# Gate and up projections in two groups of 1024 tokens, with the samples' own products and weights loaded in place

## The reference

```
x  = x + concat(A, B) @ w_out                     # one output projection
h2 = rms_norm(x, norm_ffn_w)
g, u = split(h2 @ w_ffn_in)                       # two halves of FF columns: gate and up
gc = conv_b + gp[0:T]*conv_w[0] + gp[1:T+1]*conv_w[1] + gp[2:T+2]*conv_w[2]   # gp: g behind 2 rows of history
x  = x + (silu(gc) * u) @ w_down
```

## Time and profile before

| | us |
|---|---|
| median of 3 runs (lowest, highest) | 2361.06 (2359.53, 2365.66) |
| the profiled execution's own time | 2364.47 |
| its span, first to last instruction | 2362.7 |
| before the positions | 662.4 |
| positions, to the first matmul of gate and up | 662.4 to 887.1 |
| gate and up, first group | 887.1 to 1238.7 |
| second group | 1238.7 to 1590.7 |
| third group, to the first matmul of down | 1590.7 to 1931.4 |
| down | 1931.4 to 2362.7 |

### The profile page before, as it was taken

How to read it: one execution, slowest core, us unless ns; L and a number is a source line. 1 busy time by engine, 2 the same in 40 slices (tenths; PEclk the granted TensorE clock), 3 DMA queues, 4 the chain that set the end, 5 groups by cost and what they waited for, 6 DMA issues and landing times.

```text
span 2362.7 us, 34413 instructions
## 1 busy us (share of the span) xinstructions
PE 2253.2 (95%) x13423; PEld 1984.9 (84%) x13423; DVE 1620.8 (69%) x2271; ACT 899.3 (38%) x1524; POOL 1034.6 (44%) x811
## 2 busy tenths in 40 slices
PE   7999999999999998888879999989999999999999
PEld 6899878887777888777768999988999998888887
DVE  5666655556573457888878899888998974445653
ACT  4555622222232324444444444444444433233331
POOL 4333312222121346655554666655666630245730
PEclk9999999999999998999998999999999999999999
DMA  8433222222154553444344333353333345686454
GB/s 283 151 126 121 79 86 81 81 81 67 45 183 142 192 184 122 156 139 138 132 161 140 117 118 116 118 181 100 119 118 119 119 158 190 219 289 202 139 177 165
DMA packets 208076, 333.95 MB, mean 141 GB/s; under 512 B 23083, under 2 KB 148679, under 8 KB 205847
## 3 DMA queue, kind: packets, MB, share of 16 engines
q1 hardware_dynamic: 207883, 331.69, 41.5%
q0 software_dynamic: 32, 0.07, 0.0%
HBM read 235.42 MB, written 97.24 MB: 141 GB/s over the span
## 4 chain that ended last, share of the span: by engine, by line
PE 65%; DVE 7%; DMA 5%; issue 4%; POOL 3%; ACT 3%; SPq 0%; DVEq 0%; POOLq 0%; ACTq 0%
PE bank L114 12%; PE bank L115 12%; PE bank L116 12%; PE bank L2803 9%; PE bank L2804 8%; PE bank L2805 8%; DMA late_c_raw<-in_w_ffn_in_dram 3%; DVE late_t L3184 1%; DVE late_s_act L3154 1%; DVE late_t_lo L3129 1%; POOL late_c_raw L3381 1%; POOL late_t_raw L3385 1%; DVE late_t L3187 1%; DMA late_a_raw<-h_parts 1%; ACT late_t_hi L2930 1%
## 5 line engine op out<-in xcount | busy, mean ns | idle before, releaser
L2803 PE MATMUL bank<-late_a_hi,late_b_hi 128*128 128x384 f32 (+1 forms) x1056 | 350.0, 331 | 56.3 <-issue 18.6
L2804 PE MATMUL bank<-late_a_lo,late_b_hi 128*128 128x384 f32 (+1 forms) x1056 | 344.7, 326 | 0.0
L2805 PE MATMUL bank<-late_a_hi,late_b_lo 128*128 128x384 f32 (+1 forms) x1056 | 343.2, 325 | 0.0
L2803 PE MATMUL bank<-late_a_hi,late_t_hi 128*128 128x384 f32 (+1 forms) x792 | 262.9, 332 | 19.6 <-DVE late_gp L3172 8.5
L2803 PEld LDWEIGHTS bank<-late_a_hi,late_b_hi 128*128 128x128 f32 x1056 | 201.7, 191 | 69.1 <-issue 36.3
L2804 PE MATMUL bank<-late_a_lo,late_t_hi 128*128 128x384 f32 (+1 forms) x792 | 258.3, 326 | 0.0
L2805 PE MATMUL bank<-late_a_hi,late_t_lo 128*128 128x384 f32 (+1 forms) x792 | 257.6, 325 | 0.0
L114 PE MATMUL bank<-late_e_hi,late_y_a_hi 128*128 128x512 f32 x616 | 242.1, 393 | 2.1 <-DVE late_e_lo L3202 2.1
L116 PE MATMUL bank<-late_e_hi,late_y_a_lo 128*128 128x512 f32 x616 | 242.6, 394 | 0.0
L115 PE MATMUL bank<-late_e_lo,late_y_a_hi 128*128 128x512 f32 x616 | 241.7, 392 | 0.0
L3379 POOL TENSOR_TENSOR late_t_raw<-late_c_raw 128x512 f32<-128x512 f32 x64 | 84.2, 1315 | 327.9 <-DMA late_c_raw<-in_w_ffn_in_dram 300.4
(11 more groups left out here) (380 smaller groups left out, 5187.1 us busy)
## 6 DMA issues: line engine op xcount, KB each, us to landing
late_c_raw<-in_w_ffn_in_dram SPq DMA_DIRECT2D x64, 1024.0 KB, 5.1
late_y_a_raw<-act_parts SPq DMA_DIRECT2D x77, 512.0 KB, 3.6
late_e_raw<-in_w_down_dram SPq DMA_DIRECT2D x77, 256.0 KB, 4.1
act_parts<-late_s_act SPq DMA_DIRECT2D x22, 768.0 KB, 4.4
att_next_hh<-h_parts SPq DMA_DIRECT2D x16, 1024.0 KB, 4.8
late_d_raw<-in_w_down_dram SPq DMA_DIRECT2D x11, 1024.0 KB, 7.6
late_a_raw<-h_parts SPq DMA_DIRECT2D x14, 768.0 KB, 12.7
act_parts<-late_t SPq DMA_DIRECT2D x22, 384.0 KB, 2.5
```

The lines of the kernel that those rows point to most:

```text
L2803: nc.tensor.matmul(out, w_h, hi[:, c, :], start=first, stop=False, skip_group_check=True)
L2804: nc.tensor.matmul(out, w_h, lo[:, c, :], start=False, stop=False, skip_group_check=True)
L2805: ins_ = nc.tensor.matmul(out, w_l, hi[:, c, :], start=False, stop=last, skip_group_check=True)
```

## The change

- `GROUPS` becomes two groups of 1024 prompt tokens, so H = 512 in both, and there are 22 steps and 44 units in place of 33 and 66.
- The samples are no longer columns of the first group. In each of its 22 units `sample_unit` multiplies the unit's weights with the samples' `hs_hi`, `hs_lo` plainly, behind the sixth product: 48 matmuls with 128x128 weights and 64 moving columns, into bank 6. ACT `keep_z` and DVE `add_s` take them out, and convolution, silu and gating of the samples have instructions of their own (`conv_head_s`, `tap_s`, `silu_of_s`, `gate_s`). The result goes to DRAM (`store_as`), and the samples' down projection runs in the second group, six matmuls behind the fifth product of each unit (`down_s`), with `load_as`, `load_ds`, `round_as`, `round_ds`, `split_as` and `split_ds`.
- The weights are loaded into `b_raw[u]`, which shares its memory with `b_lo[u]`. So `load_b(u, next)` waits until the unit that uses it has been multiplied (`prod`, and `prod_s` in the first group), and `split_b` waits for all four sums.
- `t` is single, and `s_act` lies over `up`: `conv_head` and the `keep_first` of u = 1 wait until the step before has been stored.
- `a_hi` of the first group lies over `w_lo` and `w_hi` of the output projection. Its rounding and splitting, seven matrices of 128x2048, move from positions 7 to 15 to the last position and into the first step, behind `w_used` and the last `proj`. `norm_x` of the last position moves behind `split_a` too.
- Tiles are stored and paired from position 9 on (4 pairs in place of 6); `first_a` moves to positions 10 to 13.

The core of the diff:

```diff
-ORDER = (0, 1, 2, 3, NT, 4, 7, 5, 8, 6, 9, 10, 13, 11, 14, 12, 15)
+ORDER = (0, 1, 2, 3, NT, 4, 5, 6, 7, 8, 12, 9, 13, 10, 14, 11, 15)
...
-GROUPS = [Group(0, 0, SAMPLE_AT * P, NS, (0, 2)), Group(1, 512, 768, 0, (2, 5)), Group(2, 1280, 768, 0, (5, 8))]
+GROUPS = [Group(0, 0, SEQ // 2, (0, 4)), Group(1, SEQ // 2, SEQ // 2, (4, 8))]
...
         def load_b(u, r):
             if r is None:
                 return
-            if turn(r) >= 1:
-                w_split(sp, before(r), 4 * u + 3)
+            p = before(r)
+            w_prod(sp, p, 7 * u + 6)
+            if has_s(p):
+                w_prod_s(sp, p, u)
...
+                p = before(r)
+                if r == FIRST:
                     store_s(final)
+                else:
+                    load_b(1, r)
+                if G.index == 1:
+                    load_ds(2 * i)
+                if has_s(p):
+                    store_as(p)
+                if G.index == 1:
+                    load_as(i)
+                store_act(p)
+                if G.index == 1:
+                    load_ds(2 * i + 1)
+                if r == LAST:
+                    load_turn(0)
+                    load_turn(1)
+                load_b(0, after(r))
...
+                if has_s(r) and n == 5:
+                    sample_unit(r, u)
+                if G.index == 1 and n == 4:
+                    down_s(2 * i + u)
...
+            for q, (b, half) in enumerate(((B11, 0), (B21, 1), (T1, 0), (B22, 1))):
+                out = s_cols(u, min(q, 2))
+                for c in range(KH):
+                    w_h, w_l = b_parts(u, b, c)
+                    n = slice((half * KH + c) * NS, (half * KH + c + 1) * NS)
+                    nc.tensor.matmul(out, w_h, hs_hi[:, n], start=q < 3 and c == 0, stop=False, skip_group_check=True)
+                    nc.tensor.matmul(out, w_h, hs_lo[:, n], start=False, stop=False, skip_group_check=True)
+                    ins_ = nc.tensor.matmul(out, w_l, hs_hi[:, n], start=False, stop=q != 2 and c == KH - 1, skip_group_check=True)
+            ins_.then_inc(prod_s, 1)
...
+                if n < 3:
+                    act.wait_ge(w_used, n + 1)
+                else:
+                    proj.wait(act, final)
...
+                w_act_out(act, p)
...
+            if has_s(p):
+                keep_z(p, 1)
             if turned:
                 round_a(G, 4)
-            if p is not None:
-                round_b(r, 1, 0)
+            if p is None:
+                round_a(G, 2)
             keep_first(r, 0, 0)
             if turned:
                 round_a(G, 5)
-            if p is not None:
-                round_b(r, 1, 1)
+            if p is None:
+                round_a(G, 3)
+                round_a(G, 4)
             keep_first(r, 0, 1)
             if turned:
+                keep_conv_s()
                 round_a(G, 6)
+            if G.index == 1:
+                round_ds(2 * i)
+                round_as(i)
             if p is None:
+                round_a(G, 5)
+                round_a(G, 6)
                 keep_h(final)
                 x_normed.wait(act, final)
-                round_b(r, 1, 0)
-                round_b(r, 1, 1)
-            round_b(r, 1, 2)
-            round_b(r, 1, 3)
-            if p is not None and p[0].sample:
-                round_d(p, 0)
-                round_acts(p)
-            if G.index == 1 and i == 0:
-                keep_conv_s()
+                round_hs()
+            for q in range(4):
+                round_b(r, 1, q)
+            if p is None:
+                keep_first(r, 1, 0)
             conv_head(r, 0)
             conv_head(r, 1)
-            keep_first(r, 1, 0)
-            round_b(nxt, 0, 0)
+            if has_s(r):
+                keep_z(r, 0)
+                conv_head_s(r)
+            if p is not None:
+                keep_first(r, 1, 0)
+            keep_first(r, 1, 1)
             silu_of(r, 0)
-            if p is not None and p[0].sample:
-                round_d(p, 1)
-            keep_first(r, 1, 1)
+            silu_of(r, 1)
+            if has_s(r):
+                silu_of_s(r)
+            if G.index == 1:
+                round_ds(2 * i + 1)
...
+            if p is final:
+                round_a(groups[0], 0)
+                round_a(groups[0], 1)
...
             if r is None:
                 return
-            if q > 1 or r == FIRST:
-                w_summed(dve, r, 4 * u + 3)
+            w_summed(dve, r, 4 * u + 3)
...
+            if has_s(p):
+                add_s(p, 1)
             if turned:
                 split_a(G, 4)
-            if p is not None:
-                split_b(r, 1, 0)
             combine(r, 0, 0)
             if turned:
                 split_a(G, 5)
-            if p is not None:
-                split_b(r, 1, 1)
+            if p is None:
+                split_a(G, 3)
+                norm_x(final)
+                split_a(G, 4)
+            sum_act(p, 0)
+            sum_act(p, 1)
             combine(r, 0, 1)
             if turned:
                 split_a(G, 6)
             if p is None:
-                split_b(r, 1, 0)
-                split_b(r, 1, 1)
+                split_a(G, 5)
+            sum_act(p, 2)
+            sum_act(p, 3)
+            if G.index == 1:
+                split_ds(2 * i)
+                split_as(i)
+            split_b(r, 1, 0)
+            combine(r, 0, 2)
+            if p is None:
+                split_a(G, 6)
+                split_hs()
+            split_b(r, 1, 1)
             split_b(r, 1, 2)
-            combine(r, 0, 2)
+            combine(r, 0, 3)
             split_b(r, 1, 3)
-            combine(r, 0, 3)
-            if p is not None and p[0].sample:
-                split_d(p, 0)
-                split_acts(p)
             combine(r, 0, 4)
-            sum_act(p, 0)
-            sum_act(p, 1)
-            if G.sample:
+            if p is None:
                 combine(r, 1, 0)
-                tap(r, 0, 1)
-                combine(r, 1, 1)
-                tap(r, 0, 2)
-                combine(r, 1, 2)
-                if p is not None:
-                    split_d(p, 1)
-                sum_act(p, 2)
-                sum_act(p, 3)
-                tap(r, 1, 1)
-                tap(r, 1, 2)
-            else:
-                tap(r, 0, 1)
+            tap(r, 0, 1)
+            tap(r, 1, 1)
+            if has_s(r):
+                add_s(r, 0)
+            if p is not None:
                 combine(r, 1, 0)
-                tap(r, 0, 2)
-                sum_act(p, 2)
-                sum_act(p, 3)
-                combine(r, 1, 1)
-                if p[0].sample:
-                    split_d(p, 1)
-                tap(r, 1, 1)
-                combine(r, 1, 2)
-                tap(r, 1, 2)
+            tap(r, 0, 2)
+            tap(r, 1, 2)
+            if has_s(r):
+                for s in (1, 2):
+                    for x in range(2):
+                        tap_s(r, x, s)
+            combine(r, 1, 1)
+            if G.index == 1:
+                split_ds(2 * i + 1)
             split_b(nxt, 0, 0)
...
             if p is final:
-                for q in range(3):
+                for q in range(4):
                     split_b(FIRST, 0, q)
+                split_a(groups[0], 0)
             add_x(p, 1)
-            if p is final:
-                split_b(FIRST, 0, 3)
             if p.c == 0:
                 ml_end.divide(dve, ml_end.last)
-            norm_x(p)
+            if p is final:
+                split_a(groups[0], 1)
+            var_x(p)
+            if p is final:
+                split_a(groups[0], 2)
+            else:
+                norm_x(p)
...
         def step(r):
             p = before(r)
-            if p is None:
-                heads(r)
-            sums_b(r, 1)
             if p is not None:
                 gate(p, 0)
                 gate(p, 1)
-                heads(r)
-            tails(r)
-            sums_b(after(r), 0)
+            if has_s(p):
+                gate_s(p)
+            heads(r)
+            sums_b(r, 1)
             if p is None:
                 pair_s(final)
+            tails(r)
+            if has_s(r):
+                tails_s(r)
+            sums_b(after(r), 0)
```

More of the change, by code:

```diff
@@ L2313, in late @@
     y_x = put("y_x", at_a, [P, 2, 2, HJ, 512])
-    y_u = put("y_u", at_a + 64 * D, [P, HJ, 512])
+    y_u = put("y_u", at_y_u, [P, HJ, 512])
+    FIRST, LAST = (groups[0], 0), (groups[-1], NP - 1)
+    positions = [Position(n) for n in range(LAST_AT + 1)]
+    final = positions[-1]
     rows_in, rows_laid, cols_laid = (k.sem(n) for n in ("rows_in", "rows_laid", "cols_laid"))
@@ L2815, in sample_down, with down_s @@
+        def down_s(n):
+            i, x = n // 2, n % 2
+            if n == 0:
+                w_sadd(pe, (groups[0], NP - 1), 1)
+                pe.wait_ge(rows_kept, 2)
+            if x == 0:
+                pe.wait_ge(acts_split, i + 2)
+            pe.wait_ge(d_split, n + 1)
```

(22 more changed lines are left out.)

484 lines of the change are left out of this document (255 added, 229 removed).

## The result

The changed kernel takes 2430.36 us (median of 4, 2423.95 to 2439.47) against 2362.86 us before (median of 4): 1.029 times as long, interval 1.025 to 1.0328. The forecast was 2354 us, the range ended at 2380.

The account below looks back on a forecast made before the run. PE alone was taken as the bound. Gate and up: stream 998.1 plus waits 3, 9, 19, 7 and 1.5 make 1037.6 us against 1044.3, 6.7 less, so 2361.1 becomes 2354 us; range 2333 to 2380.

Parts of the forecast that it names:

- The stream after the change: PE's matmuls in gate and up: 850.1 big, 117.2 samples', 30.8 samples' down, together 998.1 us, 65.3 more than before.
- 21 units of the first group: Units behind the first: steady step of two units 49.3 us, plus 3 us of waits over all eleven steps.
- Big matmuls: Gate and up: 3696 matmuls of 512 columns at 0.230 us each, 850.1 us, ends 837 and 863.
- Second group: Steady steps of 41.4 us plus 0.8 to 0.9 us waiting for down_s operands each, 9 us booked, ends 0 and 15.
- The first step: Start of gate and up: 13 us of waits for splits plus 6 us for the clock; 19 booked, ends 11 and 30.
- The positions: Before gate and up: fewer pairs, no matrices to split, first_a beside pair_s on POOL; nothing booked, ends -1 and 4.
- The change of group: From first to second group: late down_s(0), clock and transposes cost 7 us, ends 3 and 15.
- the likeliest case: Rival 1: PE's longer stream is nearly paid for by shorter waits; 2354 us, own range 2345 to 2363; 45%.
- 3: Single weight buffer's serial chain makes units with u = 0 start late; 1.5 us a step gives 2387 us; 22%.
- rival 4: Samples' loads not hidden under their matmuls, 0.14 us apart for 0.111: 31 us more, 2385 us; 5%.
- 2: Cheaper: 0.2265 us for all big matmuls, or no booked step waits, or both; 2329 to 2342 us; 20%.
- 5: No measurable change: 0.2335 us for all big matmuls, with the waits of rival 2 gone; 2361 us; 8%.

Follow-up runs that it names:

- second profile of the changed kernel: The changed kernel itself run and profiled once more beside the kernel before, nothing edited; 2429.05 us, 1.0283 of the kernel before.
- spread kernel: Changed kernel with each unit's 48 samples' matmuls dealt 12 behind each of products 2 to 5 (not the very first unit), sums in separate banks; 2378.63 us.
- e6_spread_early: Against the spread kernel, VectorE splits the samples' down operands before the third and fourth sum in the second group; 2370.43 us.
- first profile: Profiled execution of the changed kernel in its first set of runs, the slowest of four; 2439.47 us.

## Why the prediction was wrong

The step that failed is in "The stream after the change": 1056 samples' matmuls x 0.111 = 117.2 us. The distance of 0.111 us was right. Left out was that it holds at the full clock only, and that this very stretch takes the clock away, also from the product behind it. By experiment the samples cost 2378.63 - 2269.64 = 109.0 us for 45 of their 48 matmuls where the clock stays, 0.110 us each over the kernel (0.112 in a steady unit, 24.87 against 19.82 us), and 51.6 us more where it does not: some 168 us in place of 117. I had used the clock only where PE stood still, and none of the rivals had it. The kernel before gave no row on this: its only stream of few columns that I cited was six matmuls of 129 long.

The other terms, against the second profile of the changed kernel (2429.07 us, near the median), whose gate and up end at 1994.8 for a forecast 1923 before the start of down, 72 us later:

- **21 units of the first group.** Forecast 21 x 24.65 + 3 = 520.7 us, measured 573.4. In the spread kernel steady units last 24.9 and 24.8 us, so 51 of the 52.7 us too many are the clock. PE is idle for 1.1 us in all of them together (572.32 busy of 573.40): `keep_first`, the serial chain and the store are hidden as walked.
- **Big matmuls.** 0.230 us, ends 0.2265 and 0.2335. The second unit of a step in the second group has 90 matmuls of 512 columns in 20.82 us, 0.2313 each: 5 us over the kernel.
- **Second group.** Ten steps of 42.48 us, 424.8 for a forecast 422.4, `down_s` waiting as forecast. `e6_spread_early` took that wait away and got 8 of the booked 9 us.
- **The first step.** Forecast: the first product at 891.9 and the unit's end at 930.8 (924.7, and 6 for the clock). Measured 897.5 and 942.2: 11.4 us late. Half of it, 5.6 us, was late before the stage began (see the positions). The rest is in the unit: `split_hs` ends at 927.9 (these times are of the first profile; the second has them 0.3 us earlier) where I had 916.8. PE comes to the fifth product only at 914.5, when VectorE has split its matrix (one of the splits took 2.83 us where I took 2.3), and then to the transposes of the last tile in front of the sixth. ACT is idle for 4.61 us until they are done at 918.1 and only then keeps that tile and rounds the samples' rows and the weights, and VectorE is idle for 3.59 us until those weights. I had VectorE working through. Then the samples' matmuls run their whole stretch at the lower clock (10 us, distances in the timeline).
- **The positions.** I had booked nothing (ends -1 and 4) and 5 us behind them; the first product came 5.6 us later than that. In all eleven profiles with the change PE waits there for `late_o` (the mixed heads), 3.2 to 5.4 us in total, and in the kernel before 0.3. The traces show the way to it. `first_a` on POOL takes 4.6 us on 128x2048 now, and the `norm_x` that runs on VectorE beside it takes 5.6 us in place of 1.28 where POOL is idle. SP's queue has `store_x1` waiting for that `norm_x` in front of the next `late_o` load, whose last goes out at 866.4 in place of 860.4. No run moved `first_a`, so this is read and not tested. Why the first product starts at 892.5 in one profile and at 897.9 in another was not settled; the positions begin up to 6.8 us apart and last up to 4.0 us longer in one than in another.
- **The change of group.** Forecast 49.3 us for the step with 7 booked, measured 54.4: 5 more. The walk had missed the third product's wait of 2.99 us, for `combine(r, 0, 0)` behind VectorE's splits of the matrices. `down_s(0)` waits 5.2.

These make 52.7 + 11.4 + 5.1 + 2.4 (second group) = 71.6 us. At the start of down come 2 more: 3.5 us for a booked 1.5, with PE waiting 3.22 us for `late_acc_s` from VectorE. Down itself is 2.3 us shorter than before (429.0 for 431.3). The waits did shrink about as foretold: of 111.5 us before, some 45 are left (20 in the first unit, 13 at the change, 8 in the second group, 3.5 at the start of down) for 39.5 booked; some 5 of the 20 are the clock in the samples' stretch. Without the clock the kernel would still have been slower than before, at 1.006 to 1.007, outside the likeliest case's own range of 2345 to 2363 but within 2380.

Two readings were off without moving the time. VectorE's load was booked at 36 us a step and is 27.3 in both kinds of step: the splits take 8.7 us in the first group and 11.8 in the second for the booked 14, the four sums 3.7 and 3.9 for 5. So VectorE idles a third of a step and more, not a tenth to a quarter. And loads and columns of a 288-column matmul would add up to 0.11 + 0.13 us by my own price of 0.230 for 512, not 0.11 + 0.12; either is far from the 0.134 measured.

The rivals: 3 (the chain of weights: no wait of PE for late_b_lo or late_t_lo at the start of a steady unit) and 4 (loads not hidden: 0.111 us apart and not 0.14) are both refuted by the traces, so their chances for "slower" were given to mechanisms that did not act; 2 and 5 fall with the result. For rival 4 the case has a sharper row now. Matmuls of 256 columns stand 0.12 us apart with a load before each; the load's 0.11 and half of the 0.231 us of 512 columns would be 0.23 if they added up. That they add up is what the rule of the Trainium skill (page "TensorE: Matmul & The Clock Gate", section "The mechanism") would make of it, since load and matmul use the same rows. The runs do not agree with it.

## What to carry to other kernels

A stretch of matmuls with full weights and few columns can take TensorE's clock down, though the engine is busy without a gap: here 48 of 64 columns in a row did in most units, 24 in no steady unit. When such a stretch is added, look in any trace for the granted clock beside a like stretch, and if there is none, put the case "half the clock, also for what follows" among the rivals with its price. The remedy cost nothing here, where the order was free: deal the small matmuls out between the large ones (24.9 us a unit, spread or in two stretches). Then cut the number of loads, since a matmul of 64 or 128 columns cost its load, 0.11 us: operands that meet the same weights belong side by side in one matmul. And when GpSimd work is moved beside VectorE instructions, look at how long those last in the trace.

## What the runs showed of the hardware that was not expected

The clock fell with PE busy 572.32 of 573.40 us (granted 0.90 over it) and did not fall in the steady units of the same instructions in another order (24.8 to 24.9 us each). The Trainium skill, page "Perfetto Trace Analysis", section "Matmul Optimizations", asks for matmuls executed back to back in batches, because the engine scales its power with utilization; here they were back to back and in a batch, and it was the batch of narrow ones that cost. Of runs with 48 loads in a row, 64 columns each brought the clock to 0.50 (in 20 and 19 of 21 units), 128 and 256 did not. Of runs with 64 columns, 36 in a row did so once of twice, 24 in a row never in the steady units. What in the stretch the chip goes by was not measured beyond these.

At the full clock a matmul of 64 or 128 columns with its own 128x128 load takes 0.11 us of a stream, one of 256 columns 0.12 us, one of 512 columns 0.231 us. At the lower clock 64 columns take 0.21 us and 512 columns 0.42.

On VectorE the same 128x1024 instruction (`norm_x`) took 1.28 us with GpSimd idle, 2.3 us beside its sums of 128x512, and 5.6 us beside its `first_a` of 128x2048.
